# Latents stored from nine buffers in the next block, first gate weights split in the latents' projection, first request keys loaded in the gate's last item

## The reference

```python
h = rmsnorm(x, g_norm)
z = einsum('btd,de->bte', h, w_in)          # split into cq, ckv_raw, kr, z_a, ..., qc_raw, z_c, ...
q = einsum('btr,rhe->bthe', rmsnorm(cq, g_q), w_uq)
ckv = rmsnorm(ckv_raw, g_kv)                # the latents, 256 wide: an output
k_pe = rope(kr, pos)                        # the rotary keys, 32 wide: an output
o_a = attend(q[..., :64], rope(q[..., 64:], pos), ckv, k_pe)     # latent attention, 8 heads
o_c = cross_attn(qc_raw, mem_k, mem_v)      # 4 heads over 256 memory tokens of each request
o = stack([o_a * silu(z_a), o_b * silu(z_b), o_c * silu(z_c)])
```

## Time and profile before

| | us |
|---|---|
| median of three runs | 1960.88 |
| profiled execution | 1963.67 |
| its span, first to last instruction | 1961.8 |
| TensorE busy | 1853.4 (94%) |
| VectorE busy | 817.3 (42%) |
| ScalarE busy | 597.5 (30%) |
| GpSimd busy | 457.8 (23%) |

### The profile page before, as it was taken

One profiled execution on the slowest core, in us unless ns is written; L12 is line 12 of the kernel. 1 busy time (PEld: TensorE's weight loads), 2 busy tenths in 40 slices (PEclk: granted clock), 3 DMA queues, 4 the chain that ended last, 5 costly groups with the idle time before them and its releaser, 6 DMA issues. The chain is left out here.

```text
span 1961.8 us, 31675 instructions
## 1 busy us (share of the span) xinstructions
PE 1853.4 (94%) x13519; PEld 1513.4 (77%) x13519; DVE 817.3 (42%) x1523; ACT 597.5 (30%) x1174; POOL 457.8 (23%) x363
## 2 busy tenths in 40 slices
PE   5998999989999789999999999999989999999998
PEld 4644455659999446666678998999889999999986
DVE  5225466571100344445422545565552115551333
ACT  3211333442111433223302444434342223222311
POOL 0000011001220125455107600000015544454300
PEclk8999999999999889999999999999999999999999
DMA  9304000021110436845114722222143334433322
GB/s 313 160 0 165 6 12 12 1 92 43 44 44 22 155 112 223 324 153 167 50 38 102 210 64 53 53 53 53 45 117 86 82 96 142 120 85 93 108 75 86
DMA packets 193223, 189.32 MB, mean 97 GB/s; under 512 B 48285, under 2 KB 156381, under 8 KB 192957
## 3 DMA queue, kind: packets, MB, share of 16 engines
q1 hardware_dynamic: 169932, 134.13, 22.6%
q0 software_dynamic: 20592, 52.63, 9.1%
q10 hardware_dynamic: 2560, 0.56, 0.2%
HBM read 162.65 MB, written 31.92 MB: 99 GB/s over the span
## 5 line engine op out<-in xcount | busy, mean ns | idle before, releaser
L348 DVE TENSOR_SCALAR sb<-sb 128x1024 int32<-128x1024 int32 (+4 forms) x145 | 101.7, 706 | 372.4 <-DMA sb<-in_w_in 148.7
L2765 POOL TENSOR_TENSOR weights_low<-sb 128x1536 fp32r<-128x1536 f32 x42 | 148.0, 3523 | 175.9 <-DVE sb L348 175.9
L2888 PE MATMUL ps<-h_high_again,weights_high 128*128 128x272 f32 x688 | 142.3, 288 | 2.0 <-ACT weights_high L2804 2.0
L2888 PE MATMUL ps<-h_low,weights_high 128*128 128x272 f32 x688 | 142.3, 288 | 0.0
L2888 PE MATMUL ps<-h_high_again,weights_low 128*128 128x272 f32 x688 | 142.3, 288 | 0.0
L2888 PEld LDWEIGHTS ps<-h_high_again,weights_high 128*128 128x128 f32 x688 | 108.2, 188 | 2.2 <-ACT weights_high L2804 2.2
L2888 PEld LDWEIGHTS ps<-h_high_again,weights_low 128*128 128x128 f32 x688 | 108.4, 188 | 0.0
L2888 PEld LDWEIGHTS ps<-h_low,weights_high 128*128 128x128 f32 x688 | 108.3, 188 | 0.0
L2234 PE MATMUL ps<-h_high_again,recurrence_weights_high 128*128 128x384 f32 (+1 forms) x432 | 104.1, 349 | 2.2 <-ACT sb L2050 1.2
L689 POOL TENSOR_TENSOR sb<-sb 32x1088 f32<-32x1088 f32 x8 | 19.9, 2484 | 367.1 <-ACT sb L700 367.1
L1098 POOL DMA_INDIRECT sb<-in_cache_kv_latent,sb x64 | 60.6, 947 | 158.9 <-PE ps L1665 76.1
(11 more groups left out here) (347 smaller groups left out, 4047.0 us busy)
## 6 DMA issues: line engine op xcount, KB each, us to landing
sb<-in_w_in SPq DMA_DIRECT2D x82, 512.0 KB, 4.2
sb<-in_w_branch SPq DMA_DIRECT2D x48, 256.0 KB, 4.5
sb<-in_x_prompt SPq DMA_DIRECT2D x16, 512.0 KB, 4.8
values_by_level<-values POOLq DMA_DIRECT2D x56, 128.0 KB, 4.5
sb<-values_by_level POOLq DMA_DIRECT2D x7, 896.0 KB, 7.7
out<-sb SPq DMA_DIRECT2D x10, 512.0 KB, 2.8
h_low_in_dram<-h_low_staged SPq DMA_DIRECT2D x8, 544.0 KB, 3.6
h_high_in_dram<-h_high_staged SPq DMA_DIRECT2D x8, 544.0 KB, 4.3
```

The source lines that it names most:

```text
L348: return nc.vector.tensor_scalar(high.bitcast(I32), x.bitcast(I32), -4096, None, ALU.bitwise_and)
L2765: nc.gpsimd.tensor_tensor(flat(wLowR[slot]), flat(wLow[slot]), flat(wHigh[slot]), ALU.subtract)\
L2888: mm = nc.tensor.matmul(bank(4 * (k % 2) + s, n=HS2), w[:, c, :], x[:, t0:t0 + HS2], start=c == 0 and part == 0, stop=c == DC - 1 and part ...
```

## The change

Three edits.

**The stores of latents and rotary keys** move from the end of SyncE's list in the latents' projection to the head of its list in the prompt's attention. `natural` becomes nine buffers, one for each tile; three of them lie where the squares were. VectorE and ScalarE no longer wait for a buffer, and one semaphore counts all stores.

**The first two slabs of gate weights** are loaded and split in the latents' projection, behind `h`'s parts and through the same staging buffers (VectorE masks and subtracts, ScalarE rounds), and stored to DRAM (`zD`). The attention's block loads them back into the places where they are used. `split_ahead` and `gate_high` go, and the counts of the gate block's semaphores start at its third slab.

**The keys of the first four requests** are loaded by SyncE's list of the gate block, when TensorE has used the first four of eight chunks in the last item (`s_hf`); they lie over the high part of `h`, whose first four chunks are then no longer needed.

```diff
-        natural = work.take(4, KVL + ROPE)
+        natural = [work.take(KVL + ROPE) for _ in range(6)]
+        over = Arena(after_attn_in, after_attn_in + T)
+        natural += [over.take(KVL + ROPE) for _ in range(3)]
...
+        gate_raw_at = after_attn_in + 2 * T
+        gateRaw = Arena(gate_raw_at, WORDS).take(DC, 128)
...
+                def first_gate(n):
+                    sp.dma_start(gateRaw, w_cols[:, :, C_ZA + 128 * n:C_ZA + 128 * n + 128]).then_inc(s_z[n], 16)
                 for n in range(2):
                     head_weights(sp, n)
+                first_gate(0)
...
                 for n in range(2):
+                    sp.wait_ge(s_hl, DC + n + 1)
+                    if n == 0:
+                        first_gate(1)
+                    sp.dma_start(zD[1][:, n, :], lowStageR[n][:, 0:DC * 128].bitcast(F32)).then_inc(s_hd[n], 16)
+                    sp.wait_ge(s_hh, DC + n + 1)
+                    sp.dma_start(zD[0][:, n, :], highStageR[n][:, 0:DC * 128].bitcast(F32)).then_inc(s_hd[n], 16)
...
-                    if n < DC // 2:
+                    if n <= DC // 2:
                         high_part(2 * n)
                         high_part(2 * n + 1)
...
-                    if i >= 4:
-                        act.wait_ge(s_st[i % 4], 32 * (i // 4))
-                    nc.scalar.copy(natural[:, i % 4, :], bank(4 + i % 4, n=KVL + ROPE)).then_inc(s_nt_ev[1], 1)
+                    nc.scalar.copy(natural[i], bank(4 + i % 4, n=KVL + ROPE)).then_inc(s_nt_ev[1], 1)
...
+                for n in range(2):
+                    dve.wait_ge(s_hd[n], 32 * DC // 2)
+                    dve.wait_ge(s_z[n], 16)
+                    high, low = highStage[n][:, 0:DC * 128], lowStageR[n][:, 0:DC * 128]
+                    masked(high, flat(gateRaw)).then_inc(s_hm, 1)
+                    dve.wait_ge(s_hm, DC + n + 1)
+                    nc.vector.tensor_tensor(low, flat(gateRaw), high, ALU.subtract).then_inc(s_hl, 1)
...
                 for c in range(DC):
                     sp.dma_start(hLowR[c].bitcast(F32), lD[:, c, :]).then_inc(s_hr, 16)
+                for n in range(2):
+                    sp.dma_start(flat(zLowR[n]).bitcast(F32), zD[1][:, n, :]).then_inc(s_hr, 16)
...
-                    if LAST_PAIR <= g < LAST_PAIR + 6:
-                        split_ahead(g - LAST_PAIR)
...
+                sp.wait_ge(s_hf, 1)
+                for b in range(R4):
+                    request_keys(sp, b)
...
+                        if n == ITEMS4 - 1 and c == KEYS_OVER - 1:
+                            mm.then_inc(s_hf, 1)
```

More of the change, by code:

```diff
@@ L330, in build @@
         s_v2 = sem("vector_chain2")
-        s_st = [sem(f"latent_stored{i}") for i in range(4)]
+        s_st = sem("latents_stored")
         s_mst = sem("memory_stored")
@@ L360, in build @@
         lowStageR = [rounded(f"h_low_staged{i}", at, 1, T)[:, 0, :] for i, at in enumerate(low_stage_at)]
+        gate_raw_at = after_attn_in + 2 * T
+        gateRaw = Arena(gate_raw_at, WORDS).take(DC, 128)
+        zD = [nc.dram_tensor(f"gate_weights_{x}_in_dram", [128, 2, DC * 128], F32, kind="Internal").ap() for x in ("high", "low")]
+        s_z = [sem(f"gate_slab_loaded{i}") for i in range(3)]
         s_hm = sem("h_high_masked")
@@ L387, in _ @@
                     sp.dma_start(dst, (mkNat, mvNat)[n][:, :, :]).then_inc(s_mst, 16)
[L388 to L396, removed]
                 for i in range(2):
-                    sp.wait_ge(s_hd[i], 32 * DC // 2)
+                    sp.wait_ge(s_hd[i], 32 * (DC // 2 + 1))
             @block.scalar
@@ L666, in _ @@
             def _(sp):
[L667 to L670, removed]
+                for i in range(TILES + 1):
+                    rows = 128 if i < TILES else TN
+                    sp.wait_ge(s_nt_ev[i % 2], i // 2 + 1)
+                    if i < TILES:
+                        lat, pe_ = lat_p[0, 0, 128 * i:128 * i + 128, :], rope_p[0, 0, 128 * i:128 * i + 128, :]
+                    else:
+                        lat, pe_ = (a[0].rearrange("b t c -> (b t) c") for a in (lat_s, rope_s))
+                    sp.dma_start(lat, natural[i][0:rows, 0:KVL]).then_inc(s_st, 16)
+                    sp.dma_start(pe_, natural[i][0:rows, KVL:KVL + ROPE]).then_inc(s_st, 16)
                 for c in range(DC):
                     sp.dma_start(hLowR[c].bitcast(F32), lD[:, c, :]).then_inc(s_hr, 16)
+                for n in range(2):
+                    sp.dma_start(flat(zLowR[n]).bitcast(F32), zD[1][:, n, :]).then_inc(s_hr, 16)
                 for n in range(2, HA):
@@ L680, in _ @@
                     sp.dma_start(hHighR[c].bitcast(F32), hD[:, c, :]).then_inc(s_hr, 16)
-                sp.wait_ge(s_hr, 16 * 2 * DC)
+                for n in range(2):
+                    sp.dma_start(flat(zHighR[n]).bitcast(F32), zD[0][:, n, :]).then_inc(s_hr, 16)
+                sp.wait_ge(s_hr, 16 * 2 * (DC + 2))
             @block.gpsimd
@@ L710, in low @@
                     nc.scalar.copy(probT[g % 4][:, 0:k], bank(4, n=k)).then_inc(s_pa, 1)
-                def gate_high(n):
-                    act.wait_ge(s_zl, n + 1)
-                    nc.scalar.copy(flat(zHighR[n]), flat(zHigh[n])).then_inc(s_zh, 1)
                 for v in range(2 * UNITS):
                     unit(0, v)
-                for i in range(4):
-                    act.wait_ge(s_st[i], 32 * len(range(i, TILES + 1, 4)))
+                act.wait_ge(s_st, 32 * (TILES + 1))
                 act.wait_ge(s_mst, 32)
@@ L959, in _, with request_keys @@
                 attend(UNIT_STEPS // 2 - 1)
+        R4 = 4
+        work = Arena(after_mem, after_attn_in)
+        memK = work.take(R4, 2, BW)
+        memV = work.take(R4, 2, BW)
+        KEYS_OVER = -(-R4 * 2 * BW // T)
+        s_mk = [sem(f"request_memory_keys{i}") for i in range(R4)]
+        s_hf = sem("h_high_under_keys_used")
+        def request_keys(sp, b):
+            sp.dma_start(memK[:, b % R4], mem_k[0, b].rearrange("(j p) h e -> p j (h e)", p=128)).then_inc(s_mk[b % R4], 16)
         first4 = [C_ZA, C_ZB, C_QC, C_ZC]
```

44 lines of the change are left out of this document (9 added, 35 removed).

## The result

| | before | after |
|---|---|---|
| median of 7 runs each, us | 1962.51 (1955.34 to 1968.6) | 1947.02 (1937.94 to 1949.55) |
| profiled execution, us | 1963.67 | 1949.55 |
| its span, us; mean granted clock | 1961.8; 0.982 | 1947.7; 0.985 |

The changed kernel takes 0.9908 of the time before (95% interval 0.9881 to 0.9935). The forecast was 1941.0, range 1934 to 1951: the sign and the range held, and the median is 6.0 us above the forecast. The two medians of seven lie 15.5 us apart; the forecast had 19.85. The profiled execution is the longest of the seven. All ratios in this document compare fast runs; one execution of the first edit alone (2646.95 us, at a granted clock of 0.649) is slow and left out.

The account below looks back on a forecast made before the run. TensorE, busy 94% of the span, bounds the kernel; time can come from its idle 6%, its lower clock and blocks paced by other engines. Terms sum to −19.85 us: profiled 1963.67 to 1943.8, median 2.8 lower, so 1941.0; range 1934 to 1951.

Parts of the forecast that it names:

- The block's end, −5.0: End of the latents' projection: with the stores moved, the next block starts at about 173.2 instead of 178.26, −5.0 us.
- the third rival: Stores at the queue's head, one after another, hold ScalarE's first copy of values in the prompt's attention: 1981 us; chance 0.04.
- The clock behind the gap, −1.7: Start of the prompt's attention: behind TensorE's shortened gap the granted clock stays at 1.00 instead of 0.55, −1.7 us.
- The split, −5.25: Last pair of heads in the prompt's attention: without the gate split, its first six steps match the third pair's, −5.25 us.
- The bound of 3.4: Last pair of heads: only five split pieces between evacuation and next maximum are saved, −3.4 us, if the clock still falls.
- The keys, −7.9: Start of the cross-attention: four waits for request keys (5.3 us) and the slow clock behind them (2.6) go, −7.9 us.
- the second rival: A later wait for keys, values or gathers takes the cross-attention's 7.9 us back: −11.95, 1948.9 us; chance 0.10.
- the rest of the block should only be shifted: Cross-attention: second keys, their values and gathers, released by the loop's steps, move with it, keeping the −7.9 us.
- The sum: Whole kernel: −5.0 − 1.7 − 5.25 − 7.9 = −19.85 us, giving 1941.0; chance 0.58.
- the first rival: The waits go but the clock does not come back: −13.7, 1947.2 us; chance 0.25, a mixture with the forecast included.
- the 13.7: Whole kernel: gain by the waits alone, −5.0 − 3.4 − 5.3 = −13.7 us, if the clock does not come back.

Follow-up runs that it names:

- first edit alone: Only the latents' stores moved into the next block, with nine buffers, against the kernel before: 0.9984 of its time.
- first profile: The changed kernel with all three edits, first profiled execution, 1949.55 us; its runs took 0.9908 of the time before.
- second edit: Only the split of the first two gate slabs moved into the latents' projection, against the kernel before: 0.9981 of its time.
- third edit alone: Only the first request keys loaded in the gate's last item, against the kernel before: 0.9967 of its time.
- second profile: The changed kernel with all three edits, run again without further edit: 0.9923 of the time before, profiled at 1937.55 us.

## Why the prediction was right, and where it was not

**The block's end, −5.0: right.** −5.03, and the stores at the head of the next queue cost nothing (the third rival, the one on the slower side, did not come: ScalarE does not wait for them).

**The clock behind the gap, −1.7: right as a rule, not in the first profile.** Behind gaps of 6.4 us the clock was 0.55 to 0.57 in all five profiles that have one; behind 1.35 it was 1.00 in three of four (0.62 in the first profile). The attention is 262.92 with no fall and 264.71 with this one (second edit): 1.79.

**The split, −5.25: right in size, its parts mis-sized.** 26.88 to 21.64. With one fall the last pair took 25.25 (third edit alone) and with two 26.88, so a fall costs 1.63, and the split at full clock 25.25 − 1.63 − 21.64 = 2.0, an estimate. The bound of 3.4 counted the five pieces as if all of each stood in the path, and the clock had 1.85; by this estimate it is 2.0 and 3.3. The added work in the latents' projection cost nothing, as forecast: that block takes 136.57 us with it (second profile) and 136.64 without (first edit alone).

**The keys, −7.9: right for the first steps, wrong for the rest.** Steps 3 to 6 take 5.76 us (forecast 6), step 8 came 7.88 earlier, and 8.71 where no fall disturbs: 5.3 of waits, and so 3.4 of clock, where 2.6 was written. No later wait took anything back (the second rival). The sentence that failed is "the rest of the block should only be shifted": in four of the five profiles that have the third edit and no added work, a fall of 1.70 stands in the last sums, and of the four without it only the first has one there. The block goes from 85.2 to 78.3, −6.9.

**The sum: the step that failed.** It took the clock's 6.15 us (1.7, 1.85, 2.6) as gone for good, with no fall at a new place. In the profiled execution falls come back behind the gap (1.7), at the end of the third pair (some 3.3: 1.63 ahead of the first maximum and 1.65 in the next step), at the gate's start (1.44 more) and in the recurrence (3.04 more); falls near 721 and 731 are gone for 4.0. Together 5.5 of the 5.75 by which −14.1 stays behind −19.85. Both the forecast (1941.0) and the first rival (1947.2, the clock does not come back) are among what the changed kernel does: of 19 executions six lie at 1936.75 to 1939.49, seven at 1942.03 to 1945.72, six at 1946.50 to 1949.55, median 1942.92; before has 1958.2 over 66. In the mean of spans (47 and 19) the gain is 16.4: 10.8 at equal clock, and the mean clock went from 0.9856 to 0.9893, 3.7 × 1.48 = 5.5. These two shares go by the one price of the clock, which puts part of the waits down to the clock, as said above. By place, the waits that went are 5.03 + 2.0 + 5.3 = 12.3, an estimate; 1.4 of the 13.7 are missing, all of them in the split. The rest of the 16.4, some 4, is clock: less than 6.15, and spread over executions.

The Trainium skill, "TensorE: Matmul & The Clock Gate", Part 1, says that the activity watch runs free of the kernel; the three profiles of one kernel agree with that (0.62 behind the gap in the first, 1.00 in the others), though they do not show the watch itself. The prediction weighed that rule as a rival at 0.25; it should have stood inside the forecast as a spread: the 19 executions span 12.8 us. What decides the places in one execution stays open.

## What to carry to other kernels

A removed wait that ends a block or holds TensorE is worth its length, while work that another engine does between two steps may be worth less than it takes (the split: 2.0 of 3.4); the slow clock that went with it is worth its price only on the average over executions, since another fall may come elsewhere. To read a profile beside another, compare block by block between starts on the same engine: blocks that hold the same code show at once how much of a difference is clock. Before matmuls are added to hold the clock, count what one costs and whether anything ends later.

## What the runs showed that I had not expected

Without falls a block of 190 to 400 us repeats within 0.12 us. And a fall that lies in busy time can still stand behind a thin stretch: in the kernel with matmuls in seven places the clock was 0.57 from 274 to 278, with TensorE busy all the time, but only for 2.93 of the four microseconds before.

```profile
270.00:274.00 4.00, 2.93 (x13) 1.36 (x12) 3.81 (x10) 1.31 (x5) 0.00 (x0) 1.00 0.06 10
274.00:278.00 4.00, 4.00 (x15) 1.83 (x14) 2.40 (x7) 0.25 (x2) 0.00 (x0) 0.57 0.33 60
```

Not every fall does. In the kernel with fewer added matmuls the clock was 0.50 from 1141.1 on, and in the 4.1 us before it the profile has TensorE busy all the time:

```profile
1137.00:1141.10 4.10, 4.10 (x46) 4.01 (x45) 2.88 (x8) 2.69 (x8) 0.00 (x0) 1.00 0.00 0
1141.10:1144.50 3.40, 3.40 (x12) 3.40 (x12) 2.09 (x5) 2.12 (x3) 0.00 (x0) 0.50 0.00 0
```

What sets off such a fall, no run here shows.
